# Input tiles by pairs, column sums, projection, gate and taps moved in a fused two-block kernel on one core

## The reference

```python
# first block
h = rms_norm(r, g_mix);  z = h @ w_in                 # q, k, v, conv parts, gates
attn = attention(rms_norm(q), rms_norm(k), v);  conv = c_b * conv3(c_c * c_x)
r = r + (sigmoid(g_a) * (attn @ w_attn_out) + sigmoid(g_c) * (conv @ w_conv_out)) @ w_o
r = r + square(relu(rms_norm(r, g_mlp) @ w_up)) @ w_down
r = r + sigmoid(rms_norm(r, g_ple) @ w_ple_gate) * (p @ w_ple_proj)
# second block: 16 meta tokens go before the 256
u = rms_norm(h, norm_mix_pre) @ conv_w_in + b_in;  a, g = split(u)
u = conv31(a * sigmoid(g)) + b_dw;  u = silu(layer_norm(u)) @ conv_w_out + b_out
h = h + rms_norm(u);  h = h + rms_norm(swiglu(rms_norm(h)));  return h[16:]
```

## Time and profile before

| what | us |
|---|---|
| median of 3 runs | 2592.4 |
| lowest, highest | 2590.39, 2595.18 |
| profiled execution | 2591.07 |
| its span | 2588.8 |

### The profile page before, as it was taken

The page is one execution under the profiler, slowest core; times in us unless marked ns, Lnnn a source line. Parts: engine busy times, 40 slices in busy tenths (PEclk is TensorE's granted clock), DMA queues, the critical chain, the costliest instruction groups (busy, mean ns, idle before and its releaser), DMA issues.

```text
span 2588.8 us, 43837 instructions
## 1 busy us (share of the span) xinstructions
PE 2540.1 (98%) x14943; PEld 2248.4 (87%) x14943; DVE 1756.0 (68%) x2120; ACT 1273.7 (49%) x1604; POOL 459.2 (18%) x300
## 2 busy tenths in 40 slices
PE   8999999999999999999999999989899999999998
PEld 7888788888888888888888899978788888888887
DVE  6578875577765665665667879985766556665665
ACT  5456555554544444444445544454654444444444
POOL 4034410001100000000011268862400000000003
PEclk9999999999999999999999999999999999999999
DMA  6655456665566665566655555536466656666653
GB/s 199 202 174 172 147 185 193 189 193 179 170 187 195 189 190 188 180 198 189 187 185 179 179 157 161 163 94 205 140 195 184 195 179 194 193 188 188 190 181 130
DMA packets 497408, 465.27 MB, mean 180 GB/s; under 512 B 14476, under 2 KB 494214, under 8 KB 497286
## 3 DMA queue, kind: packets, MB, share of 16 engines
q1 hardware_dynamic: 496816, 463.92, 58.0%
q10 hardware_dynamic: 516, 0.38, 0.1%
HBM read 462.15 MB, written 2.10 MB: 179 GB/s over the span
## 4 chain that ended last, share of the span: by engine, by line
PE 91%; DVE 4%; issue 2%; ACT 1%; POOL 1%; DVEq 0%; ACTq 0%; POOLq 0%
PE gp L396 54%; PE gp L399 25%; PE gp L405 3%; PE gp L588 2%; PE gp L590 2%; PE gp L589 2%; DVE wlo L1195 1%; POOL acc L1739 1%; PE xp L606 1%; POOL sq L1736 0%; DVE xp L1517 0%; ACT whi L718 0%; PE xp L633 0%; DVE s L1206 0%; DVE s L1474 0%
## 5 line engine op out<-in xcount | busy, mean ns | idle before, releaser
L1195 DVE TENSOR_TENSOR wlo<-stage,whi 128x1024 fp32r<-128x1024 f32 x811 | 1014.1, 1266 | 674.0 <-ACT whi L718 667.4
L718 ACT ACTIVATE whi<-stage 128x1024 fp32r<-128x1024 f32 x876 | 915.7, 1057 | 967.3 <-PE gp L399 723.8
L396 PE MATMUL gp<-A,whi 128*128 128x512 f32 x3968 | 1315.8, 394 | 7.0 <-DVE A L1598 7.0
L399 PE MATMUL gp<-A,wlo 128*128 128x256 f32 x3200 | 898.7, 281 | 0.0
L396 PEld LDWEIGHTS gp<-A,whi 128*128 128x128 f32 x3968 | 741.2, 188 | 170.1 <-issue 8.1
L396 PE MATMUL gp<-B,whi 128*128 128x512 f32 x2496 | 872.1, 394 | 9.6 <-DVE B L1568 7.9
L399 PE MATMUL gp<-B,wlo 128*128 128x256 f32 x2496 | 700.1, 280 | 0.0
L399 PEld LDWEIGHTS gp<-A,wlo 128*128 128x128 f32 x3200 | 604.3, 189 | 0.0
L396 PEld LDWEIGHTS gp<-B,whi 128*128 128x128 f32 x2496 | 468.1, 188 | 116.5 <-issue 10.2
L399 PEld LDWEIGHTS gp<-B,wlo 128*128 128x128 f32 x2496 | 472.4, 189 | 0.1
L1736 POOL TENSOR_TENSOR sq<-r 128x512 f32 (+1 forms) x32 | 38.9, 1215 | 814.6 <-DVE r L1427 756.4
(11 more groups left out here) (289 smaller groups left out, 1418.9 us busy)
## 6 DMA issues: line engine op xcount, KB each, us to landing
stage<-in_w_in SPq DMA_DIRECT2D x160, 512.0 KB, 4.6
stage<-in_w_up SPq DMA_DIRECT2D x128, 512.0 KB, 3.8
stage<-in_w_down SPq DMA_DIRECT2D x128, 512.0 KB, 4.2
stage<-in_ffn_w_gate SPq DMA_DIRECT2D x88, 512.0 KB, 4.5
stage<-in_ffn_w_up SPq DMA_DIRECT2D x88, 512.0 KB, 4.5
stage<-in_ffn_w_down SPq DMA_DIRECT2D x88, 512.0 KB, 4.5
stage<-in_conv_w_in SPq DMA_DIRECT2D x64, 512.0 KB, 4.1
stage<-in_w_o SPq DMA_DIRECT2D x32, 512.0 KB, 4.5
```

The source lines that it names most:

```text
L396: nc.tensor.matmul(bank.rearrange("p (a t) -> p a t", a=2), hi, both_parts(M, kt), start=first, stop=False)
L399: done = nc.tensor.matmul(bank[:, T:2 * T], lo, M[:, kt, 0:T], start=False, stop=last)
L718: nc.scalar.activation(whi[:, slot, :], stage[:, slot, :], ACT.Copy).then_inc(hi_ready, 1)
L1195: nc.vector.tensor_tensor(wlo[:, slot, :], stage[:, slot, :], whi[:, slot, :].bitcast(F32), ALU.subtract).then_inc(lo_ready, 1)
```

## The change

- The start: TensorE waits for three constants in place of four, and runs some matmuls of `ones` into an unused bank (`keep_busy`). A quarter of x is handed on in two pairs of tiles. Quarters 1 to 3 are turned behind the high matmuls of units 0 to 2. ScalarE takes the first pair of x before unit 0's weights, and VectorE takes a quarter's low parts before the weights'.
- `column_sums(0)` stands behind unit 3 of its body in place of unit 0.
- The projection runs 12 matmuls of 256 columns per pair into one region, and ScalarE alone copies it to `PP`; its 8 pairs no longer count among the pairs of `plan`, and use a semaphore of their own (`ple_out`).
- The gate: VectorE writes the low part of the pair before while the sigmoid runs. The last body is written out, and the conversion of its last unit stands behind the last tail.
- conv2: the taps of tile 0 stand behind unit 2 of pair 1, in place of unit 1; the centre sum stands behind unit 3 of pair 6.

```diff
@@ plan
-        hp += n
+        hp += 0 if name == "ple" else n
@@ TensorE
-            pe.wait_ge(consts, 4)
+            def keep_busy(n, bank):
+                for _ in range(n):
+                    nc.tensor.matmul(bank[:, 0:P], ones, ones, start=True, stop=True)
+            pe.wait_ge(consts, 3)
+            keep_busy(4, gp[:, 0, :])
             pe.wait_ge(gain_loaded, 16)
...
-                done.then_inc(x_turned, 1)
+                    if kk % 2:
+                        done.then_inc(x_turned, 1)
+            keep_busy(2, gp[:, 0, :])
             turn_x(0)
-            turn_x(1)
+            keep_busy(4, gp[:, 0, :])
...
-            body("qkv", 0, A, h1, {0: [lambda: turn_x(2)], 1: [lambda: turn_x(3)]}, hi_first=True)
-            body("qkv", 1, A, h1, {0: [lambda: column_sums(0)]}, hi_first=True)
+            body("qkv", 0, A, h1, hi_first=True, mid={c: lambda c=c: turn_x(c + 1) for c in range(3)})
+            body("qkv", 1, A, h1, {3: [lambda: column_sums(0)]}, hi_first=True)
...
                 for j in range(2):
-                    pe.wait_ge(evacuated, XSLOTS + hp0 + 2 * u + j - 1)
-                    for k in range(2):
-                        for m in range(2):
+                    pair = 2 * u + j
+                    if pair < 4:
+                        pe.wait_ge(evacuated, XSLOTS + hp0 - 1 + pair // 2)
+                    else:
+                        pe.wait_ge(ple_out, pair - 3)
+                    for m in range(2):
+                        o = gp[:, pair % 4, m * T:m * T + T]
+                        for k in range(2):
                             c = k * 512 + (2 * j + m) * P
-                            nc.tensor.matmul(gp[:, 2 * j + m, :], whi[:, u, c:c + P], pT[:, k, :],
-                                             start=(k == 0), stop=False)
-                            done = nc.tensor.matmul(gp[:, 2 * j + m, T:2 * T], wlo[:, u, c:c + P], pT[:, k, 0:T],
-                                                    start=False, stop=(k == 1))
+                            nc.tensor.matmul(o, whi[:, u, c:c + P], pT[:, k, 0:T], start=(k == 0), stop=False)
+                            nc.tensor.matmul(o, whi[:, u, c:c + P], pT[:, k, T:2 * T], start=False, stop=False)
+                            done = nc.tensor.matmul(o, wlo[:, u, c:c + P], pT[:, k, 0:T], start=False, stop=(k == 1))
                     done.then_inc([ple_half, unit_used][j], 1)
             column_sums(1)
+            pe.wait_ge(ple_out, 8)
...
-                conv2(i, i % 2, {1: [taps(i - 1, (i - 1) % 2, free=i >= 3)], 2: [sum_for_centre] if i == 6 else []})
+                conv2(i, i % 2, {2 if i == 1 else 1: [taps(i - 1, (i - 1) % 2, free=i >= 3)],
+                                 3: [sum_for_centre] if i == 6 else []})
@@ ScalarE
+            hi_of_x(0, 0)
             take_hi(0, 0, 0)
-            hi_of_x(0)
-            take_hi(1, 0, 1)
-            hi_of_x(1)
-            copy_x(0)
...
+            hi_of_x(0, 1)
+            for c in range(1, 4):
+                take_hi(c, 0, c)
+                hi_of_x(c, 0)
+                hi_of_x(c, 1)
+                copy_x(c - 1)
             copy_x(3)
...
-                take_cross(hp0 + 2 * u, 0, None, (ple_half, u + 1))
-                take_cross(hp0 + 2 * u + 1, 1, n0 + u + 1)
+                for j in range(2):
+                    pair = 2 * u + j
+                    act.wait_ge(*[(ple_half, u + 1), (unit_used, n0 + u + 1)][j])
+                    nc.scalar.activation(PP[:, 2 * pair:2 * pair + 2, :], gp[:, pair % 4, :].rearrange("p (m t) -> p m t", m=2),
+                                         ACT.Copy).then_inc(ple_out, 1)
                 take_hi(n0 + u + RING, n0 // RING + 1, u)
...
-            with act.Fori(1, 4) as it:
+            with act.Fori(1, 3) as it:
                 body("gate", it, gate_tail)
+            n, q, hp0 = at["gate"][1] + 24, at["gate"][1] // RING + 6, at["gate"][0]
+            convert(n, q)
+            take_cross(hp0 + 6, 0, n + 4)
+            gate_tail(3, 0)
+            n, q = n + 4, q + 1
+            convert(n, q, 3)
+            take_cross(hp0 + 7, 1, n + 4)
+            gate_tail(3, 1)
+            take_hi(n + RING + 3, q + 1, 3)
@@ VectorE
             for c in range(4):
-                take_lo(c, c)
                 for kk in range(4):
...
+                take_lo(c, c)
...
             for u in range(4):
-                for j in range(2):
-                    add_up(hp0 + 2 * u + j, j, PP[:, 4 * u + 2 * j:4 * u + 2 * j + 2, :])
                 take_lo(n0 + u + RING, u)
...
                 nc.vector.tensor_tensor(t, t, by_rstd(), ALU.mult).then_inc(gate_normed, 1)
+                if j or not isinstance(it, int) or it:
+                    lo_of_r(16, A, "mix_pre", h - 1, META)
                 dve.wait_ge(gate_sig, h + 1)
...
-                lo_of_r(16, A, "mix_pre", h, META)
...
-            with dve.Fori(1, 4) as it:
+            with dve.Fori(1, 3) as it:
                 body("gate", it, gate_tail)
+            n = at["gate"][1] + 24
+            convert(n)
+            gate_tail(at["gate"][0] + 6, 3, 0)
+            convert(n + 4, 3)
+            gate_tail(at["gate"][0] + 7, 3, 1)
+            lo_of_r(16, A, "mix_pre", 7, META)
+            take_lo(n + 4 + RING + 3, 3)
```

More of the change, by code:

```diff
@@ L234, in two_block_kernel @@
         late_turned, late_hi, p_ready, ple_half = sem("late_turned"), sem("late_hi"), sem("p_ready"), sem("ple_half")
+        ple_out = sem("ple_out")
         meta_step, meta_sum, meta_var, meta_act = sem("meta_step"), sem("meta_sum"), sem("meta_var"), sem("meta_act")
@@ L377, in _, with step @@
         def _(pe):
-            def step(hp, j, n0, M, kt0=0, units=4, slot0=0, ready=None, after=None, single=False, hi_first=False):
+            def step(hp, j, n0, M, kt0=0, units=4, slot0=0, ready=None, after=None, single=False, hi_first=False, mid=None):
                 for u in range(units):
@@ L399, in step @@
                                 done = nc.tensor.matmul(bank[:, T:2 * T], lo, M[:, kt, 0:T], start=False, stop=last)
+                    if mid and u in mid:
+                        mid[u]()
                     if hi_first:
@@ L410, in step, with body @@
                             f()
-            def body(phase, it, M, ready, hooks=None, kt0=0, single=False, hi_first=False):
+            def body(phase, it, M, ready, hooks=None, kt0=0, single=False, hi_first=False, mid=None):
                 hp0, n0 = at[phase]
@@ L417, in body @@
                     step(hp0 + 2 * it + j, j, n0 + 8 * it + 4 * j, M, kt0, ready=ready, after=after,
-                         single=single and j == 0, hi_first=hi_first)
+                         single=single and j == 0, hi_first=hi_first, mid=mid if j == 0 else None)
             def column_sums(k, last=0):
@@ L777, in _, with hi_of_x @@
             act.wait_ge(vec_ready, 1)
-            def hi_of_x(c):
-                act.wait_ge(x_turned, c + 1)
-                for kk in range(4):
+            def hi_of_x(c, half):
+                act.wait_ge(x_turned, 2 * c + half + 1)
+                for kk in (2 * half, 2 * half + 1):
                     nc.scalar.activation(A[:, 4 * c + kk, 0:T], x_home(c)[:, kk, :], ACT.Copy,
@@ L787, in copy_x @@
                 nc.scalar.activation(r[:, 4 * c:4 * c + 4, :], x_home(c), ACT.Copy).then_inc(evacuated, 1)
+            hi_of_x(0, 0)
             take_hi(0, 0, 0)
-            hi_of_x(0)
-            take_hi(1, 0, 1)
-            hi_of_x(1)
-            copy_x(0)
-            take_hi(2, 0, 2)
-            hi_of_x(2)
-            copy_x(1)
-            take_hi(3, 0, 3)
-            hi_of_x(3)
-            copy_x(2)
+            hi_of_x(0, 1)
[4 more added lines that the diff above has]
+                copy_x(c - 1)
             copy_x(3)
@@ L1478, in gate_tail @@
                 nc.vector.tensor_tensor(rr, rr, t, ALU.add).then_inc(r_updated, 1)
-                lo_of_r(16, A, "mix_pre", h, META)
+            dve.wait_ge(ple_out, 8)
             body("gate", 0, gate_tail, {2: [lambda: variance(2, 2, RMS_EPS)]})
-            with dve.Fori(1, 4) as it:
+            with dve.Fori(1, 3) as it:
                 body("gate", it, gate_tail)
+            n = at["gate"][1] + 24
[5 more added lines that the diff above has]
+            take_lo(n + 4 + RING + 3, 3)
             variance(3, 3, RMS_EPS)
```

## The result

The changed kernel takes 2578.83 us (median of 5 runs, 2576.23 to 2580.54), where the kernel before takes 2592.40 on the same chip (5 runs, 2590.28 to 2595.18). The ratio is 0.9946, with an interval from 0.9935 to 0.9958: 13.6 us faster, where 10.8 was forecast. The time lies in the predicted range. The profiled execution took 2578.83 us for a span of 2577.0.

What follows compares the result with a forecast made beforehand. TensorE was taken as the bound, busy 98% of the span, so only its idle or half-speed times could gain. +1.3 + 0 - 3.9 - 1.1 - 1.2 - 5.9 = -10.8 us, from 2592.4 to 2581.6; range 2574.5 to 2587.

Steps and rivals of the forecast that it cites:

- The start, +1.3: Start of the kernel: turning each quarter of x behind the high matmuls exposes a wait per unit, 1.3 us lost.
- the loop: Start: transposes, ScalarE's high part, VectorE's low part and matmuls in turn, 4.5 us a unit against 3.6 of TensorE work.
- Column sums, 0: Column sums three units later: the 3.40 us wait for GpSimd goes, but later waits replace it, 0 gained.
- the collision stays: Units 14 to 16: unit 14's load still lands late beside the tap weights' load; unit 16 comes 1.3 us late, past 65.
- they collide less: Rival: unit 14's load escapes the tap weights or collides less, most of 5.3 us is kept; about 2575.5, chance 0.17.
- Projection, -3.9: The p projection in one region: VectorE's addition and the single cross buffer's waits go, 3.9 us gained.
- Gate, -1.1: Gate stage: low parts leave the path of a 1.69 us stall, of which about 0.6 stays; 1.1 us gained.
- Last gate unit, -1.2: Last gate unit converted after the tail: the last two tiles of A come about 2 us earlier, 1.2 us gained.
- Taps, -5.9: conv2's taps one unit later: the 3.26 us wait and the clock's fall behind it (2.7 us) go, 5.9 us gained.
- VectorE's lag: conv2: VectorE lags TensorE by 2.7 us from the earlier taps and takes it up by the last pair.
- VectorE holds conv2: Rival: TensorE meets VectorE's lag in conv2 and only 3.2 us stay; 2584.3, chance 0.13.
- is caught by GpSimd: Rival: GpSimd slows VectorE once in each of conv2's 14 pairs, 1.9 us each, 26 in all; 2608, chance 0.03.

Runs made afterwards that it cites:

- the experiment: The changed kernel, with TensorE waiting for 6 of the projection's 8 copies ahead of the column sums, not all 8 behind them: 2576.90 us, 0.9947.
- the two repeats: The changed kernel and the kernel before, each run once more unaltered: 2575.25 and 2591.84 us; their second theory: the pace is dealt out anew in each execution.

## Why the prediction was right, by its own steps

- **The start, +1.3.** Right: +1.57 at unit 4 (+1.2 by the means over several profiles), the loop, its period and the first matmul within 0.3 us. The `ones` matmuls cost nothing and the clock held: from unit 1 on a unit's 8 high matmuls last 2.02 to 2.10 us, and those of unit 0, in two groups, 1.15 and 1.19. Whether the `ones` matmuls raised it, no run shows.
- **Column sums, 0.** The step that failed reads: "Both shift by the start's 1.5 us, so the collision stays, and unit 16 comes 1.3 us late, past 65." The collision stayed: unit 15's load took 14.0 us. But unit 14 and not unit 15 was taken as the late one, from one profile, and it is the one whose delay varies. The two issues did not shift alike either: against the first profile the tap weights came 1.33 us later (40.14), unit 14's load 0.53 (39.64), and their order turned round. When unit 14 lands first, the variance and the reciprocal of the norm leave the chain, and unit 16 is 5.1 us behind unit 15's landing. It measured -4.77 us in the first profile, -2.8 by the means. The rival "they collide less" had this mechanism and 0.17; its 2575.5 does not follow from its own terms, which give 2576.3 (5.3 off the 2581.6).
  The Trainium skill's "DMA: Bandwidth & Descriptors" (section "Why a DMA increments its semaphore by 16 and not by 1") has the outer dimension divided over the engines, so that 31 rows go to one and 16 rows to 16. The two runs with 16 and 15 rows agree: unit 14's 14.0 us became 4.7. The rule was right on what collides. The prediction drew too much from it: that the column sums were then worth 0.
- **Projection, -3.9.** The mechanism was right, two terms of the sum were too small. A matmul of 256 columns costs 0.120 us here, not 0.116 (680.56 to 680.68), so a pair takes 1.44 us, not 1.40: 0.3 us over eight pairs. The wait for `ple_out` behind the column sums leaves the entry of up0's loop bare: 0.69 us in the profile, 1.04 by the experiment. With them -2.76 against -3.9 is explained to 0.2 us. The prediction had the wait in the diff and gave it no price: it put up0 0.2 us behind the end of the last copy (684.2 to 684.4), and it is 0.9 us (681.48 to 682.39).
- **Gate, -1.1.** The sign was right, the size was not: the term "about 0.6 stays" of the stall measured 1.19, so that 0.5 us go (0.4 over the stage). The -1.17 of the marks is this and 0.7 us of TensorE's faster pace in the first profile.
- **Last gate unit, -1.2.** Right: -1.57 in the change, and 1.36 lost when taken out again.
- **Taps, -5.9.** Right: -5.65 in the change and -5.63 alone, clock included, both against the first profile. The 2.7 us for the low clock were taken from that profile, where it lasted long; by the means the edit is worth 5.3. VectorE's lag is there from pair 2 and gone at pair 7, without cost, as worked out. The rivals that VectorE holds conv2 or is caught by GpSimd are refuted by its pairs 12.48 us apart.
- **Not forecast:** stretches with unchanged code. See the last section; they gave +2.7 us in this profile, and -0.7 within the gate.

The six edits sum to -14.35 in the marks, against the forecast -10.8. With the means (start +1.2, column sums -2.8, taps -5.3) and the gate at -0.5 they are -11.7, and with the -1.65 of up0 -13.4, where the medians differ by 13.6. So the forecast total was near for a reason that is partly luck: the column sums gave 2.8 us that it denied them, and the projection and the gate 1.7 and the taps 0.6 less than it gave them.

## What to carry to other kernels

A gap on the bounding engine hides others behind it: before crediting its removal, name what is late next, and read that lateness from more than one profile where a transfer is in it, since the same kernel had 4.7 and 14.9 us for one load. A wait right ahead of a loop is not free because its event comes before the engine runs dry: what the sequencer still has to do behind it, here 0.9 us, is then bare. Ask for no more than the loop's first writes need, and ahead of other work of that engine. A transfer whose row count does not divide well (here 31 rows of 8 KB, one after another for 12.5 us) holds back the loads beside it; cut it into pieces that are spread (here 16 and 15).

## What the runs showed of the hardware

**TensorE has two paces at full granted clock.** In out2, the same code and data, the mean of one 128x512 matmul that reads `B`, in a window from 1740 to 1825: kernel before, before again, after, after again.

```profile
L396 PE MATMUL gp<-B,whi 128*128 128x512 f32 x240 | 83.2, 391 | 0.0
```

```profile
L396 PE MATMUL gp<-B,whi 128*128 128x512 f32 x238 | 84.1, 399 | 0.0
```

```profile
L397 PE MATMUL gp<-B,whi 128*128 128x512 f32 x195 | 68.9, 399 | 0.0
```

```profile
L397 PE MATMUL gp<-B,whi 128*128 128x512 f32 x195 | 67.6, 391 | 0.0
```

At 391 ns a unit takes 2.773 us, at 399 it takes 2.830, 2% more, and the granted clock is 1.00 in both. The pace holds over long runs of units, often a whole stage, and most of its changes stand at a restart. Over all twelve profiles the stages' lengths fall into groups (us between first matmuls):

```
stretch               kernels with the old projection       with the new projection
up0 to gate           713.4 to 713.6  (6 of 6)              711.8 to 711.9  (6 of 6)
out2 to glu0          100.1 (2), 101.5 to 101.9 (4)         100.1 to 100.3 (3), 101.5 to 102.0 (3)
glu0 to the end       748.4 (5), 750.8 (1)                  748.4 (4), 750.8 (2)
```

The first row belongs to the change: with the old projection up0's first units run at the slow pace each time, with the new one at the fast, 1.65 us that no step of the prediction had. Start, column sums and taps, each alone, left it slow; the projection's edit was not run alone. The other two rows are dealt out anew in each execution, of the same kernel too: the changed kernel has 748.41 in its second profile and 750.84 in its first. That was the second theory of the two repeats. Its sign, 2 us or more from out2 to the end, came in the changed kernel (852.8 and 848.5) and not in the kernel before (848.5 and 850.0), where out2 alone changed its pace. These two rows make the 4.3 us that the marks lose behind conv2, and part of the 3 to 5 us by which the runs of one kernel differ. What sets the pace stays open; no experiment here isolated it.

**The same stop, with and without a fall of the clock.** Between 285 and 328 us TensorE stands twice for 1.5 and then 0.8 us in every profile. In five of the twelve the granted clock falls to 0.50 at one of these stops, in seven it does not. From 286 to 296 us its mean is 1.00 in the first profile of the changed kernel, 0.83 in the one with two loads of tap weights, and 0.93 in the second of the kernel before. With such a fall the stretch from unit 16 to the projection takes 608.9 to 609.2 us, without it 607.7 to 607.9. So what a stop costs behind itself is not to be read from one profile either.

**One load, two fates.** Unit 14's load takes 4.3 or 14.9 us in kernels whose issues stand within 1 us of each other. What decides between them, the nine profiles do not tell; the load behind it is late in every case in which the tap weights are one load. At 0.5 us ahead of the tap weights, anything from 5.4 to 14.0 us was seen.
